# The two branch products by one level of Strassen's scheme, with their weights in the attention's ring slots

## The reference, cut to what matters

```python
h = rmsnorm(x, g_mix)
u = h @ w_in                     # 512 pool channels | q | k | v
y_a = pool_mixer(u_pool, w_pool_mix, pool_scale) @ w_branch_a   # (512 x 512) @ (512 x 1024)
y_b = swa_attention(q, k, v, ...) @ w_branch_b                  # (512 x 512) @ (512 x 1024)
gates = sigmoid(h @ w_gate + b_gate)                            # 512 x 2048
merged = gates[:, :1024] * y_a + gates[:, 1024:] * y_b
x = x + merged @ w_out
h2 = rmsnorm(x, g_ffn)           # then router, 64 experts (top 8), shared expert, a last gated sum
```

## Time and profile before

| | |
|---|---|
| time, median of 3 runs | 996.32 us (993.3 to 997.54) |
| the profiled execution's own time | 995.38 us |
| its span, first to last instruction | 993.5 us |
| busy share of the span: PE, DVE, ACT, POOL | 95%, 34%, 16%, 20% |
| mean granted TensorE clock | 0.986 |
| chain that ended last: PE, DMA | 76%, 18% |
| DMA over the span | 301.03 MB, mean 303 GB/s |

### The profile page before, as it was taken

The page is one execution under the profiler, slowest core; times in us unless marked ns, Lnnn a source line. Parts: engine busy times, 40 slices in busy tenths (PEclk is TensorE's granted clock), DMA queues, the critical chain, the costliest instruction groups (busy, mean ns, idle before and its releaser), DMA issues.

```text
span 993.5 us, 15496 instructions
## 1 busy us (share of the span) xinstructions
PE 941.1 (95%) x6263; PEld 465.7 (47%) x6263; DVE 339.4 (34%) x749; ACT 162.6 (16%) x304; POOL 201.4 (20%) x332
## 2 busy tenths in 40 slices
PE   6999999999999999999999999999979898997698
PEld 4578888854446533333333333354323332332344
DVE  5565673222226753333332111111101111111687
ACT  2001334120011211111111111111101112121021
POOL 4115923000010102222222222212121211101210
PEclk9999999999999999999999999999989999999799
DMA  9940002265362599999999999999999999999972
GB/s 331 326 128 1 1 1 85 85 201 180 105 288 75 195 385 373 410 416 401 393 418 415 414 419 414 410 423 415 405 422 422 422 420 421 414 400 361 368 274 84
DMA packets 83911, 301.03 MB, mean 303 GB/s; under 512 B 9299, under 2 KB 35959, under 8 KB 59648
## 3 DMA queue, kind: packets, MB, share of 16 engines
q1 hardware_dynamic: 71200, 264.24, 67.7%
q0 software_dynamic: 11920, 33.63, 8.7%
q10 hardware_dynamic: 720, 2.16, 0.5%
HBM read 279.26 MB, written 29.36 MB: 311 GB/s over the span
## 4 chain that ended last, share of the span: by engine, by line
PE 76%; DMA 18%; DVE 2%; SPq 2%; issue 1%; ACT 1%; DVEq 0%; POOL 0%; ACTq 0%
PE ps L2105 22%; DMA ring<-in_w_exp_up 16%; PE ps L1721 12%; PE ps L2134 9%; PE ps L1860 6%; PE ps L2247 5%; PE ps L1677 3%; PE ps L1844 3%; PE ps L1842 3%; PE ps L1654 2%; DMA ring<-in_w_exp_down 2%; PE ps L1931 1%; PE ps L1683 1%; PE ps L2114 1%; SPq L514 1%; SPq L500 1%
## 5 line engine op out<-in xcount | busy, mean ns | idle before, releaser
L2105 PE MATMUL ps<-ring,gates 128*32 128x512 f32 x2560 | 288.8, 603 | 26.1 <-DMA ring<-in_w_exp_up 25.4
L2105 PEld LDWEIGHTS ps<-ring,gates 128*32 128x32 f32 x2560 | 87.6, 111 | 219.0 <-issue 218.1
L2134 PE MATMUL ps<-ring,poolbuf 128*32 128x512 f32 x1280 | 147.3, 601 | 3.0 <-DMA ring<-in_w_exp_down 2.1
L1482 DVE COPY poolbuf<-ps 128x256 f32<-128x256 f32 x40 | 17.0, 424 | 356.2 <-PE ps L2114 356.2
L747 POOL TENSOR_TENSOR tickets<-cst 128x1 f32<-128x1 f32 x77 | 14.5, 188 | 398.2 <-ACT actT L946 392.7
L2134 PEld LDWEIGHTS ps<-ring,poolbuf 128*32 128x32 f32 x1280 | 38.3, 110 | 84.7 <-issue 83.0
L946 ACT ACTIVATE actT<-ps,qT 128x1024 f32<-128x1024 f32 x40 | 44.5, 1113 | 143.9 <-PE ps L2134 143.9
L938 ACT ACTIVATE poolbuf<-ps 128x256 f32<-128x256 f32 x40 | 15.3, 384 | 279.3 <-PE ps L2105 279.3
L1721 PE MATMUL ps<-xrow,ring 128*128 128x256 f32 x256 | 57.9, 381 | 0.1
L1860 PE MATMUL ps<-ring,gates 128*128 128x512 f32 x128 | 56.4, 594 | 0.0
L1654 PE MATMUL ps<-cst,rows 128*128 128x128 f32 x352 | 48.5, 285 | 7.6 <-DVE rows L1035 7.6
(11 more groups left out here) (269 smaller groups left out, 1001.3 us busy)
## 6 DMA issues: line engine op xcount, KB each, us to landing
ring<-in_w_exp_down SPq DMA_DIRECT2D x64, 1024.0 KB
ring<-in_w_exp_gate SPq DMA_DIRECT2D x62, 1024.0 KB, 10.8
ring<-in_w_exp_up SPq DMA_DIRECT2D x62, 1024.0 KB, 18.9
ring<-accumulator SPq DMA_DIRECT2D x12, 1024.0 KB, 12.5
ring<-in_w_gate SPq DMA_DIRECT2D x8, 1024.0 KB, 10.1
ring<-in_w_in SPq DMA_DIRECT2D x5, 1024.0 KB, 13.0
xrow<-in_x SPq DMA_DIRECT2D x8, 512.0 KB, 7.5
accumulator<-ring SPq DMA_DIRECT2D x1, 4096.0 KB, 19.6
```

What stands on the lines that cost most here:

```text
L2105: last = mm(bank(2 + k)[part, :], hgT[k][:, q, part], pair_view(EXPERT_SLOT[js[c]])[:, q], start=(q == 0), stop=(q == KD - 1))
L2134: last = mm(bank(6 + half)[part, :], eactT[r % 2][:, q, part], w[:, q, half * 512:(half + 1) * 512], start=(q == 0), stop=(q == 1))
```

## The change

Both branch products are done by the same scheme in 28 phases c = 0 to 27 (`branch_phase`): 7 for each of y_a and y_b, for each of two halves p of the output channels. A phase has 4 matmuls of 256 columns into one of four banks, and DVE adds it into a quadrant of `branch_out` (`branch_sum`), which takes over `xrow` and ring slots 7 and 0. Sums of weights are made on POOL after phase 20 (`branch_weight_sums`), sums of activations on DVE after the gate sums 21 and 23 (`input_sums`, into `rows`). POOL multiplies y_a by its gate (`scale_ya`), and DVE multiplies y_b by its gate and adds (`merge`), at four places. `mix` moves from behind phase 25 to behind phase 19. The branch weights are loaded into slots 8 to 11. The second load of `x` waits for `merged_ready` 2, and the shared expert's weights and all that follow wait for `merged_ready` 4. `out_proj` takes its chunks in another order. The semaphore `gate_copied` is now `phase_summed`.

```diff
-    ["wa0", "wb0", "wa1", "wb1"] + [f"out{c}" for c in range(4)] + ["shg", "shu"]
-DENSE_SLOT = [u % 8 for u in range(17)] + [1, 2, 3, 4, 6, 7]
+    ["wa0", "wa1", "wb0", "wb1"] + [f"out{c}" for c in range(4)] + ["shg", "shu"]
+DENSE_SLOT = [u % 8 for u in range(13)] + [8, 9, 10, 11] + [1, 2, 3, 4, 6, 7]
+K_ORDER = [0, 1, 4, 5, 2, 3, 6, 7]
...
+            attention_done = {8: (score_read, 4 * NT), 9: (probT_ps, 4 * NT), 10: (attn_ps, NT), 11: (mix_ps, NG)}
...
-            sp.wait_ge(gate_ps, PHASES)
+            sp.wait_ge(merged_ready, 2)
             for i in range(NT):
                 sp.dma_start(xrow[:, i, :], x_rows[i]).then_inc(x_loaded[i], 16)
+            sp.wait_ge(merged_ready, 4)
             for u in range(DENSE_AT["shg"], N_DENSE):
                 load_dense(u)
-            sp.wait_ge(merged_ready, KD)
...
+            def branch_weight_sums(b):
+                for h in range(2):
+                    pool.wait_ge(slot_loaded[DENSE_SLOT[DENSE_AT[f"w{'ab'[b]}{h}"]]], 16)
+                w11, w12, w21, w22 = branch_quarters(b)
+                t1, t2, t4 = branch_wsums[b]
+                for n, (dst, x, y) in enumerate(((t1, w12, w11), (t2, w22, t1), (w12, w22, w12), (t4, w21, t2))):
+                    nc.gpsimd.tensor_tensor(dst, x, y, ALU.subtract).then_inc(wsum_ready, 1)
+                    pool.wait_ge(wsum_ready, 4 * (PAIRS + 1) + 4 * b + n + 1)
+
+            def scale_ya(p):
+                pool.wait_ge(phase_summed, PHASES + 14 * p + 7)
+                pool.wait_ge(gates_ready, 2 * KD)
+                for h in range(2):
+                    at = gates[:, 4 * h + 2 * p:4 * h + 2 * p + 2, :]
+                    nc.gpsimd.tensor_tensor(at, at, branch_out[2 * p][:, h], ALU.mult).then_inc(ya_scaled, 1)
+
+            pool.wait_ge(gate_ps, 21)
+            branch_weight_sums(0)
+            branch_weight_sums(1)
+            scale_ya(0)
+            scale_ya(1)
...
+            def input_sums(b):
+                if b == 0:
+                    dve.wait_ge(mixed_ready, NG)
+                else:
+                    dve.wait_ge(attn_ready, NT)
+                b11, b12, b21, b22 = branch_inputs(b)
+                s = mix_sums[b]
+                for n, (dst, x, y, op) in enumerate(((s[0], b21, b22, ALU.add), (s[1], s[0], b11, ALU.subtract),
+                                                     (s[2], b11, b21, ALU.subtract), (s[3], b12, s[1], ALU.subtract))):
+                    nc.vector.tensor_tensor(dst, x, y, op).then_inc(hsum_ready, 1)
+                    dve.wait_ge(hsum_ready, 4 + 4 * b + n + 1)
+
             for q in range(4 * NT + 4, PHASES):
                 gate_sum(q)
...
+                if q in (21, 23):
+                    input_sums((q - 21) // 2)
...
+            def merge(p, h, done):
+                ga, gb = (gates[:, half * KD + 4 * h + 2 * p:half * KD + 4 * h + 2 * p + 2, :] for half in range(2))
+                dve.wait_ge(phase_summed, PHASES + done)
+                dve.wait_ge(gates_ready, 2 * KD)
+                link(nc.vector.tensor_tensor(gb, gb, branch_out[2 * p + 1][:, h], ALU.mult))
+                dve.wait_ge(ya_scaled, 2 * p + h + 1)
+                nc.vector.tensor_tensor(ga, ga, gb, ALU.add).then_inc(merged_ready, 1)
...
+            mix()
+            for q in range(4 * NT + 4, PHASES):
                 gate_phase(q)
...
+            def branch_phase(c):
...
+                if c >= 4:
+                    pe.wait_ge(phase_summed, PHASES + c - 3)
...
+                for f in range(2):
+                    for k in range(2):
+                        last = mm(bank(2 + c % 4)[:, f * HALF_T:(f + 1) * HALF_T],
+                                  w[:, k, (2 * p + f) * P:(2 * p + f + 1) * P], x[:, k, :],
+                                  start=(k == 0), stop=(k == 1))
...
-            out_proj(0, 0)
-            out_proj(0, 1)
+            out_proj(0, 0, 0, 4)
+            out_proj(0, 1, 0, 4)
+            out_proj(0, 0, 4, 8)
+            out_proj(0, 1, 4, 8)
```

More of the change, by code:

```diff
@@ L406, in quadrant, with branch_quarters, branch_inputs @@
             return gates[:, c:c + 2, token_half * HALF_T:(token_half + 1) * HALF_T]
+        mix_sums = [[rows[:, 2 * b:2 * b + 2, :].rearrange("p i n -> p (i n)")[:, n * 512:(n + 1) * 512].rearrange(
+            "p (k n) -> p k n", k=2) for n in range(4)] for b in range(2)]
+        branch_wsums = [[v.rearrange("p (k n) -> p k n", k=2) for v in flat] for flat in (
+            (ring[:, 5, 0:D], ring[:, 5, D:2 * D], ring[:, 6, 0:D]),
+            (ring[:, 6, D:2 * D], ka[:, 0:D], poolbuf[:, NG * (T + PAD):NG * (T + PAD) + D]))]
+        branch_out = [v.rearrange("p (h f n) -> p h f n", h=2, f=2) for v in (
+            xrow[:, 0:2, :].rearrange("p i n -> p (i n)"), xrow[:, 2:4, :].rearrange("p i n -> p (i n)"),
+            ring[:, 7, :], ring[:, 0, :])]
+        def branch_quarters(b):
+            first, second = (unit_view(DENSE_SLOT[DENSE_AT[f"w{'ab'[b]}{h}"]], 4) for h in range(2))
+            return first[:, 0:2, :], second[:, 0:2, :], first[:, 2:4, :], second[:, 2:4, :]
+        def branch_inputs(b):
+            src = (mixedT, qT)[b]
+            return [src[:, 2 * c:2 * c + 2, t * HALF_T:(t + 1) * HALF_T] for t in range(2) for c in range(2)]
         def pair_view(slot):
@@ L878, in _ @@
             act.wait_ge(vec_ready, 1)
-            for p in range(PAIRS - 1):
+            for p in range(PAIRS - 2):
                 gate_sigmoids(p)
@@ L1091, in phase_sum, with add_phase @@
             def phase_sum(p, n, done):
-                c11, c12, c21, c22 = (quadrant(p, t, h) for t in range(2) for h in range(2))
+                return add_phase([quadrant(p, t, h) for t in range(2) for h in range(2)], n, done)
+            def add_phase(quadrants, n, done):
+                c11, c12, c21, c22 = quadrants
                 done = done.rearrange("p (f n) -> p f n", f=2)
@@ new lines, in branch_sum @@
+            def branch_sum(c):
+                j, n = c // 7, c % 7
+                dve.wait_ge(branch_ps, c + 1)
+                dve.wait_ge(phase_summed, PHASES + c)
+                c11, c12, c21, c22 = (branch_out[j][:, h, :, t * HALF_T:(t + 1) * HALF_T]
+                                      for t in range(2) for h in range(2))
+                add_phase((c11, c12, c21, c22), n, bank(2 + c % 4)).then_inc(phase_summed, 1)
+            def merge(p, h, done):
[5 more added lines that the diff above has]
+                nc.vector.tensor_tensor(ga, ga, gb, ALU.add).then_inc(merged_ready, 1)
@@ L1227, in residual @@
+            for c in range(BRANCH_PHASES):
+                branch_sum(c)
+                if c == 14:
+                    merge(0, 0, c + 1)
+                if c == 16:
+                    merge(0, 1, c + 1)
+                if c == BRANCH_PHASES - 2:
+                    merge(1, 0, c + 1)
+            merge(1, 1, BRANCH_PHASES)
             def residual(i, half):
@@ L1821, in _ @@
                 gate_phase(4 * n + 7)
-            for q in range(4 * NT + 4, PHASES - 2):
+            mix()
+            for q in range(4 * NT + 4, PHASES):
                 gate_phase(q)
[L1824 to L1836, removed]
+            def branch_phase(c):
+                j, n = c // 7, c % 7
+                p, b = j // 2, j % 2
+                if n == 0 and p == 0:
+                    loaded(f"w{'ab'[b]}0")
+                    loaded(f"w{'ab'[b]}1")
@@ L1837, in _ @@
                     pe.wait_ge(mixed_ready, NG)
                     pe.wait_ge(attn_ready, NT)
[L1839 to L1845, removed]
@@ L1846, in _ @@
-                    last.then_inc(branch_ps, 1)
+                if n == 1 and p == 0:
+                    pe.wait_ge(hsum_ready, 8 + 4 * b)
+                if n in (1, 3, 5) and p == 0:
+                    pe.wait_ge(wsum_ready, 4 * (PAIRS + 1) + 4 * b + (2, 3, 4)[n // 2])
+                if c >= 4:
+                    pe.wait_ge(phase_summed, PHASES + c - 3)
+                w11, w12, w21, w22 = branch_quarters(b)
+                t1, t2, t4 = branch_wsums[b]
+                b11, b12, b21, b22 = branch_inputs(b)
@@ L1848, in out_proj @@
+            for c in range(BRANCH_PHASES):
+                branch_phase(c)
             def out_proj(i, half, k0=0, k1=KD):
@@ L1856, in out_proj @@
                 w = pair_view(DENSE_SLOT[DENSE_AT[f"out{2 * half}"]])
-                for k in range(k0, k1):
+                for n in range(k0, k1):
                     if i == 0 and half == 0:
-                        pe.wait_ge(merged_ready, k + 1)
-                    last = mm(bank(half), gates[:, k, i * P:(i + 1) * P], w[:, k], start=(k == 0),
-                              stop=(k == KD - 1))
+                        pe.wait_ge(merged_ready, n // 2 + 1)
+                    k = K_ORDER[n]
+                    last = mm(bank(half), gates[:, k, i * P:(i + 1) * P], w[:, k], start=(n == 0),
+                              stop=(n == KD - 1))
                 if k1 == KD:
```

31 lines of the change are left out of this document (16 added, 15 removed).

## The result

| | |
|---|---|
| time of the changed kernel, median of 20 runs | 998.28 us (995.89 to 999.83) |
| time of the kernel before, median of 20 runs beside it | 996.37 us (993.3 to 998.07) |
| ratio | 1.0016, 95% interval 1.0009 to 1.0024 |
| the profiled execution: span, mean granted clock | 997.6 us, 0.981 |

The change makes no difference of 0.5%, as forecast. The median of 998.28 us lies inside the stated range of 989.0 to 999.5, 1.6 us above the likeliest value of 996.7. The changed kernel is slower by 1.6 us as the ratio has it, where +0.4 us was forecast. The size alone would not say whether nothing happened or two things cancelled, so the rows come next.

A forecast was written before the change was run, and what follows sets the result against it. PE was taken to bound the front part from 201 to 290 us, so changes before 345 us reach the end in full. Terms -6.5 and +6.9 gave +0.4 us on 996.3, forecast 996.7 us, range 989.0 to 999.5.

The forecast's parts named there:

- Term 1: Branch products on PE: 224 records at a pitch of 0.216 us take 48.4 us instead of 54.93, so -6.5 us.
- Term 2: Last gate phases: DVE's input sums alternate with POOL's weight sums, 2.9 us a turn, delaying phase 26 on PE: +6.9 us.
- The clock: PE phases 24 and 25: the 4.5 us stall makes them 1.7 us longer, hidden because PE would otherwise idle before phase 26.
- The 6.3 that the prediction called a floor: Term 2 with a turn of 2.8 us, the least delay as long as the turns alternate.
- The signs: Expected profile: lengthened input and weight sums, PE idle before phases 24 and 26, branch products near 215 us, `out_proj` near 263.4.
- The loads: Four `mid_loaded` loads behind merge 4: landing at 284 to 286.6 us, slack 2 to 5 us, costed at nothing.
- (c): Rival: late `mid_loaded` loads delay L1239, the residual and PE; a landing at 295 us reaches 1001.5 us; chance 0.07.
- The sum: Terms 1 and 2 together, -6.5 + 6.9 = +0.4 us on the median of before, 996.3, giving 996.7 us.
- (a): Rival: DVE and POOL don't alternate in the gate phases, term 2 is 0, time 989.8 us (989 to 991); chance 0.18.
- (b): Rival: alternation for one product only, just the first stall of 4.5 us and 1.7 of clock, 991 to 995 us; chance 0.10.
- the 998.7 worked out with a turn of 3.17 us: Estimate by the skill's SBUF page, no overlap within a DVE and POOL turn: term 2 about 8.9 us, time near 998.7.

The follow-up runs named there:

- the version with the sums early: Changed kernel with all eight DVE input sums made ahead of gate sum 20 and POOL's start: 990.33 us, ratio 0.9929; on another chip 991.05 us, 0.9938.
- the three kernels above: Changed kernel with POOL's weight sums waiting for all input sums (991.77 us), with all input sums ahead of POOL (990.33), with memsets for POOL's sums (3059).
- two steps of 3 MB above: All input sums early, plus the four `mid_loaded` loads issued behind 3 MB of expert weights (991.17 us), then behind 6 MB (1000.02 us).
- the two kernels with one group early: Changed kernel with only y_b's four input sums moved ahead of POOL's start (996.91 us, ratio 1.0008), or only y_a's (996.87 us, 1.0004).

## Why the prediction was right

**Term 1, the 28 phases on PE**: -6.5 forecast, -6.58 measured, and the pitch of 0.216 us from the gate phases held (48.35 us for 224 records, as worked out). No wait in the branch phases, as forecast; DVE's second merge and the tail behind the last phase were covered.

**Term 2, DVE and POOL in turns**: +6.9 forecast. Phase 26 starts at 207.71; in the version with the sums early the same place is at 180.53 + 6 x 3.454 = 201.25, or 201.4 with the start 0.1 us later of the changed kernel. That makes +6.3 at this place. The two phases behind it take 7.14 us on the chain and not 6.91, so the branch products start 6.6 us late by it (34.20 - 27.63). The mechanism is shown by the three kernels above: it needs both engines at the same time, and it needs POOL to read SBUF, as far as a memset can stand for an operation that doesn't. The gate sums, with an input in PSUM, weren't held (1.48 us for two). The turn was 2.75 us where 2.9 was taken and 2.8 was the lower bound. Phase 24 started at 198.71 (forecast 198.8), the idle time before it was 4.25 (4.5). Gate sum 24 ended at 207.57 (208.1).

**The clock**: the two phases behind the first wait were longer by 1.8 us (forecast 1.7), and this was hidden almost wholly by the second wait (0.17 us left, forecast 0.7). The 6.3 that the prediction called a floor was what came out at phase 26. One execution of the changed kernel went past that: its branch products start 0.4 us later (215.26), by the clock alone. The prediction took the idle times of 2.23 us (a loss) and 1.77 us (none) for the two sides of a limit; the length alone doesn't decide it, as the rows in the last section show. Nothing in the sum hung on that.

**The signs**: seven of the eight input sums took 1.33 to 2.73 us (1.2 to 2.9 forecast), POOL's sums up to 2.69 (up to 3), the branch products began at 214.85 (near 215) and `out_proj` at 263.20 (near 263.4).

**The loads**: the last of the four landed at 280.8 us; the prediction had 284 to 286.6. It took 12.9 us from the first issue before and 12.9 after, with 3.3 MB issued in place of 2.3. The rate that the prediction scaled was too low: before, the four were issued 2 us behind the first load, and the experts' loads issued from 268.88 us on shared the DMA with them, so that it moved 3.7 MB in those 12.9 us (288 GB/s). Bytes count all the same: two steps of 3 MB above moved the landing by 8.2 and 7.1 us. The slack was 8.7 us and not 2 to 5. Costing the loads at nothing was right, the rival's distance was too short. A landing 27 us after the issue would also not have been half of the rate seen before, as rival (c) has it, but 0.12 MB/us against 0.18.

**The sum**: the chains give -6.58 + 6.57, and 0.15 us because the kernel reaches this stretch later: +0.14 us, forecast +0.4. The time came out 1.6, 1.0 and 0.8 us above before in three sets, two of whose intervals include no difference. What is above 0.14 us is in none of the terms forecast. In the profiles it can only arise after 349 us, and there one execution differs from the next by more than it: in the three profiles of the changed kernel the last wait for `w_exp_up` ends at 883.70, 882.54 and 880.14 us, in the one of before at 880.70. The early wait at 530.56 is no mark of this kernel either, since a faster version, with the sums early, had one at 523.96. Whether the rest of about 1 us belongs to the kernel is open. The versions that separate the two engines have the same expert stage and gain 6.6 us on the chain, and 6.4, 7.1 and 6.2 us in the times (5.1 with 3 MB ahead of the loads). Their intervals reach 1.4 to 2 us to either side, so they can't settle it.

**The rivals**: (a), no alternation, is what the kernel gets when the two engines are kept apart: 990.3 to 991.8, forecast 989.8. So the value given to it was the right price for the right condition; the condition was not met. (b), alternation for one product only, was priced too low: 991 to 995 was forecast, and the two kernels with one group early took 996.9. The prediction's own 4.5 us of waiting and 1.7 of clock already make 996.3 - 6.5 + 6.2 = 996.0. That the second wait adds next to nothing it had seen for its main case, and not for this rival. (c) is the case of the late loads above.

**What the number alone is worth**: little. The range of 989.0 to 999.5 holds the prices of (a) and (b) too, so a time inside it doesn't choose between them. It is the waits in the profile, and the kernels that take them away, that bear the forecast out. That 998.28 lies nearer to the 998.7 worked out with a turn of 3.17 us than to 996.7 is chance: the turn was 2.75.

## What to carry to other kernels

Before work is moved to POOL, list the DVE operations of the same stretch that read two SBUF tensors, and see who waits for what is queued behind them; if POOL's operations read SBUF too, count full turns of both (here 2.75 us for 0.69 of work). One change of order, on either engine, made this change worth 0.6 to 0.7% in place of nothing: the version with the input sums ahead of POOL's start beats both kernels, at 990.3 to 991.1 us. And a stall that follows another is not a second sum to add or to win back: removing either half of the cause here won nothing, removing both won all of it.

## What the hardware showed that I had not expected

- POOL's memset of 128x1024 and DVE's two-input sums ran side by side at 0.95 and 0.69 us, where POOL's subtraction and the same sums took turns of 2.75 us.
- A turn is shorter than the two operations one after the other (2.75 against 0.69 + 2.36 = 3.05): about 0.3 us of each pair overlaps.
- The loss to the clock behind PE's idle time of 4.24 to 4.62 us was 1.8, 2.75, 2.5 and 1.8 us in four profiles (the changed kernel twice, then with one half early and with the other), at a granted 0.73, 0.60, 0.66 and 0.66 in a stretch of 5 us there. Behind 6.64 us of idle time it was 2.5, at 0.50.
- The longer of two short idle times can be the harmless one. Both rows are from the profile of the changed kernel, with a granted clock of 1.00 from 641 to 646 us and of 0.66 from 656 to 661:

```profile
641.41 7.07 PE L2194 MATMUL ps<-ring,gates 128*32 128x512 f32 x64 [2.31 <-DMA ring<-in_w_exp_up]
656.30 8.77 PE L2194 MATMUL ps<-ring,gates 128*32 128x512 f32 x64 [1.90 <-DMA ring<-in_w_exp_up]
```
